# Weight block sums of two down products kept in DRAM, one pair sum moved between two taps, and the joints' order changed, in a kernel of two transformer blocks

## The reference, cut to what matters

```python
# first block (SiLU gate), then a gated per-layer embedding ("ple")
h = rms_norm(x, norm_ffn)
x = x + (silu(h @ w_ffn_gate) * (h @ w_ffn_up)) @ w_ffn_down
gate = sigmoid(rms_norm(x, norm_ple) @ w_ple_gate)
x = x + gate * (p @ w_ple_proj)
x = rms_norm(x, norm_final)
# second block (a causal depthwise convolution of 3 taps, GELU gate)
u = causal_dwconv(h2 @ w_up, conv_w, conv_b)
y = (gelu(u[..., :2816]) * u[..., 2816:]) @ w_down
```

## Time and profile before

| | us |
|---|---|
| median of 3 runs | 2708.07 (2702.29 to 2712.51) |
| the profiled execution, its own time | 2705.71 |
| its span | 2703.9 |
| PE busy | 2583.1 (96%), 11826 matmuls |
| DVE busy | 1786.3 (66%) |
| ACT busy | 1189.3 (44%) |
| POOL busy | 1199.0 (44%) |
| chain that ended last, by engine | PE 56%, DVE 22%, ACT 6%, POOL 6%, DMA 5%, issue 5% |

### The profile page before, as it was taken

The page is one execution under the profiler, slowest core; times in us unless marked ns, Lnnn a source line. Parts: engine busy times, 40 slices in busy tenths (PEclk is TensorE's granted clock), DMA queues, the critical chain, the costliest instruction groups (busy, mean ns, idle before and its releaser), DMA issues.

```text
span 2703.9 us, 32099 instructions
## 1 busy us (share of the span) xinstructions
PE 2583.1 (96%) x11826; PEld 2081.1 (77%) x11826; DVE 1786.3 (66%) x2176; ACT 1189.3 (44%) x2076; POOL 1199.0 (44%) x764
## 2 busy tenths in 40 slices
PE   7999999999899999999898999998999999999997
PEld 6887788888688888888676777877767777777875
DVE  6888876653855454589945556427378666666997
ACT  6777421122533333444454243355354444444444
POOL 2444522223455555556633311134433555554566
PEclk9999999999999999999999999999999999999998
DMA  3000044432122222565422112122321222226753
GB/s 123 24 24 24 19 149 155 153 113 109 47 79 85 86 78 94 170 232 176 144 78 89 48 31 46 32 76 69 132 86 63 78 86 71 86 78 221 253 177 132
DMA packets 119580, 271.59 MB, mean 100 GB/s; under 512 B 12664, under 2 KB 26232, under 8 KB 119296
## 3 DMA queue, kind: packets, MB, share of 16 engines
q1 hardware_dynamic: 119424, 269.54, 30.1%
HBM read 231.15 MB, written 38.34 MB: 100 GB/s over the span
## 4 chain that ended last, share of the span: by engine, by line
PE 56%; DVE 22%; ACT 6%; POOL 6%; DMA 5%; issue 5%; SPq 0%; DVEq 0%; ACTq 0%; POOLq 0%
PE psum_mem L750 20%; PE psum_mem L1045 15%; PE psum_mem L1075 4%; POOL w_lo L3958 3%; DVE tmp_mem L3672 3%; DMA w_raw<-in_w_up_b 2%; PE psum_mem L1244 2%; PE psum_mem L1249 2%; PE psum_mem L1246 2%; PE psum_mem L812 2%; DVE x_lo_a L3065 2%; DVE w_raw L2942 1%; PE psum_mem L796 1%; DVE w_raw L3048 1%; PE psum_mem L847 1%
## 5 line engine op out<-in xcount | busy, mean ns | idle before, releaser
L3958 POOL TENSOR_TENSOR w_lo<-w_raw,w_hi 128x512 fp32r<-128x512 f32 x320 | 495.9, 1555 | 464.2 <-ACT w_hi L1834 447.6
L3864 POOL TENSOR_TENSOR w_lo<-w_raw,w_hi 128x1024 fp32r<-128x1024 f32 (+2 forms) x105 | 237.4, 2261 | 624.5 <-ACT w_hi L1599 542.0
L1834 ACT CAST w_hi<-w_raw 128x512 fp32r<-128x512 f32 x320 | 196.4, 620 | 323.2 <-DMA w_raw<-in_w_up_b 72.1
L1045 PE MATMUL psum_mem<-h_hi,w_hi 128*128 128x512 f32 x672 | 266.4, 396 | 20.9 <-ACT norm_row L2470 18.2
L1045 PE MATMUL psum_mem<-h_lo,w_hi 128*128 128x512 f32 x672 | 264.0, 393 | 1.3 <-DVE h_lo L2951 1.3
L1045 PE MATMUL psum_mem<-h_hi,w_lo 128*128 128x512 f32 x672 | 263.2, 392 | 0.0
L750 PE MATMUL psum_mem<-h_hi,w_hi 128*128 128x512 f32 x736 | 232.1, 397 | 11.4 <-ACT h_hi L1633 8.9
L750 PE MATMUL psum_mem<-h_lo,w_hi 128*128 128x512 f32 x736 | 228.8, 392 | 5.7 <-DVE h_lo L3582 5.5
L750 PE MATMUL psum_mem<-h_hi,w_lo 128*128 128x512 f32 x736 | 228.3, 391 | 2.7 <-POOL w_lo L3864 2.7
L1599 ACT CAST w_hi<-w_raw 128x1024 fp32r<-128x1024 f32 (+2 forms) x105 | 100.3, 955 | 266.9 <-PE psum_mem L750 253.8
L750 PEld LDWEIGHTS psum_mem<-h_hi,w_hi 128*128 128x128 f32 x736 | 137.9, 189 | 43.4 <-ACT h_hi L1633 8.9
(11 more groups left out here) (466 smaller groups left out, 6434.1 us busy)
## 6 DMA issues: line engine op xcount, KB each, us to landing
hidden<-tmp_mem SPq DMA_DIRECT2D x44, 512.0 KB, 2.6
w_raw<-in_w_up_b SPq DMA_DIRECT2D x44, 512.0 KB, 3.7
w_raw<-in_w_ffn_down SPq DMA_DIRECT2D x77, 256.0 KB, 3.4
w_raw<-in_w_down_b SPq DMA_DIRECT2D x77, 256.0 KB, 3.2
x_ring_a<-hidden SPq DMA_DIRECT2D x66, 256.0 KB, 3.3
x_ring_b<-hidden SPq DMA_DIRECT2D x66, 256.0 KB, 3.2
w_raw<-in_w_in_a SPq DMA_DIRECT2D x32, 512.0 KB, 3.7
ada_raw<-in_w_ada SPq DMA_DIRECT2D x64, 256.0 KB, 3.3
```

Of the source, the lines that this page charges most:

```text
L1045: made = e.matmul(out, wt, x, start=j <= DIFF_3 and k == 0 and part == 0, stop=k == KH - 1 and part == 2, skip_group_check=True)
L1834: e.copy(w_slot(w_hi, slot, of), source).then_inc(*S.of("w_hi", key))
L3864: e.tensor_tensor(w_lo[:, i, 0:width], w_raw[:, i, 0:width], w_hi[:, i, 0:width].bitcast(F32), ALU.subtract).then_inc(*S.of("w_lo", c))
L3958: e.tensor_tensor(w_slot(w_lo, slot, of), source, w_slot(w_hi, slot, of).bitcast(F32), ALU.subtract).then_inc(*S.of("w_lo", key))
```

## The change

1. The weight sums of M_6, M_7, M_3 and M_5 of both down products are made during the first block's feed-forward pairs: 22 tile groups (11 for "a", 11 for "b"), one beside each of the pairs 1 to 19, two beside the pairs 1, 7 and 13. Each takes two loads of 512 KB, four DVE sums of 128x512 and one store of 1 MB to a new DRAM scratch array `down_sums`. Two DVE sums stand ahead of the pair sum, two behind the high weight sum. `keep_w`, its 22 loads and the weight part of `down_sums` are gone; the four products read their weight tiles from the array.
2. Both down products use the order M_1, M_2, M_5, M_6, M_7, M_4, M_3.
3. In the second block DVE's pair sum of pair i+1 moves between the two up taps of pair i, the high weight sum of pair i+1 behind the second tap, and the product of pair i behind that. Unit 3 of the second down product is prepared one step earlier.
4. In the joint, the ple rows are made in halves as soon as their blocks are final: first half of rows 0 to 3 beside M_6, the rest beside M_3, and the last four after it. ACT's split of p's weight tile moves behind all of these rows. The small gain vectors move to unit 15.
5. `hidden_out(KF - 1)` moves behind the weight load of unit 6, in both down products.

```diff
-DOWN_ORDER = {"a": (M_1, M_2, M_5, M_6, M_3, M_7, M_4), "b": (M_1, M_2, M_5, M_6, M_7, M_4, M_3)}
+DOWN_ORDER = (M_1, M_2, M_5, M_6, M_7, M_4, M_3)
+W_SUM = {M_6: 0, M_7: 1, M_3: 2, M_5: 3}
+SUM_TILES = [(of, kt) for of in "ab" for kt in range(KF // 2)]
+def sum_tiles_beside(i):
+    return [n for n in range(len(SUM_TILES)) if 1 + n * 19 // len(SUM_TILES) == i]
...
 ACT, first block, down product
             for u in range(2, DOWN_UNITS):
                 p, kt = divmod(u, KB)
...
-                if p == 6 and kt in (0, 2, 4, 6):
...
+                if p == 3 and kt in (0, 2, 4, 6):
+                    if kt == 0:
+                        for n in (KF - 2, KF - 1):
+                            w.wait_ge(f"hid_out{n % 2}", ("a", n))
+                    ple_row(kt // 2, 0)
+                elif p == 6 and kt < 4:
+                    ple_row(KH + kt, 1)
+                elif p == 6 and 6 <= kt < 10:
+                    ple_row(KH + kt - 6, 0)
+            for k in range(KH):
+                ple_row(k, 1)
             ahead(1)
-            for k in range(KH, KD):
-                w.wait_ge(*down_added("a", 6, k - KH))
...
 ACT, second block, pairs
                 tap_first(i, 1, up_banks(i))
+                if i == KF - 1:
+                    down_unit("b", 3)
                 gelu(i)
...
 DVE, down_sums
-                if m in W_KEPT + W_MADE:
...
-                        e.tensor_tensor(kept, kept, raw, ALU.add).then_inc(*S.of("dn_sum", (of, "w", u)))
...
 DVE, first block, pairs
+            def first_tile_sums(n):
+                low, high, late, high_late = (sum_part(n, j) for j in range(4))
+                w.wait_ge(f"in_ws{n % 2}", (n, 1))
+                e.tensor_tensor(high_late, high, high_late, ALU.add).then_inc(*S.of("ws_sum", (n, M_5)))
+                w.own("ws_sum")
+                e.tensor_tensor(high, low, high, ALU.subtract).then_inc(*S.of("ws_sum", (n, M_7)))
+
+            def last_tile_sums(n):
+                low, high, late, high_late = (sum_part(n, j) for j in range(4))
+                w.own("ws_sum")
+                e.tensor_tensor(low, high_late, low, ALU.subtract).then_inc(*S.of("ws_sum", (n, M_6)))
+                w.own("ws_sum")
+                e.tensor_tensor(late, late, low, ALU.subtract).then_inc(*S.of("ws_sum", (n, M_3)))
             for _, i in FFN_PAIRS:
+                for n in sum_tiles_beside(i):
+                    first_tile_sums(n)
...
                 b_sum(i)
...
                 weight_high_sum(i)
+                for n in sum_tiles_beside(i):
+                    last_tile_sums(n)
...
 DVE, second block, pairs
+            back_sum(PLAIN)
+            weight_high_sum(PLAIN, "b")
             for _, i in FFN_PAIRS[PLAIN:]:
-                back_sum(i)
-                weight_high_sum(i, "b")
...
-                whole_rest(i, 1, up_banks(i))
+                late_taps = tap_rest(i, 1, up_banks(i))
+                next(late_taps)
+                if i < KF - 1:
+                    back_sum(i + 1)
+                else:
+                    down_low("b", 3)
+                for _ in late_taps:
+                    pass
+                if i < KF - 1:
+                    weight_high_sum(i + 1, "b")
                 ffn_product(i)
...
 SP, w_load
+                if m in W_SUM:
+                    n = SUM_TILES.index((of, kt))
+                    w.wait_ge(f"ws_out{n % 2}", n)
+                    source = io["down_sums"][n][:, HALF * W_SUM[m]:HALF * (W_SUM[m] + 1)]
...
 SP, first block, pairs
+                for n in sum_tiles_beside(i - 1):
+                    sum_out(n)
+                for n in sum_tiles_beside(i):
+                    sum_load(n)
...
 SP, both down products
-            hidden_out("a", KF - 1)
             for u in range(4, DOWN_UNITS):
                 w_load("a", u)
+                if u == 6:
+                    hidden_out("a", KF - 1)
                 if u >= KB:
                     x_load("a", u)
-                if u < KB + 4:
-                    kept_w_load("a", u - 4)
```

More of the change, by code:

```diff
@@ L1140, in tensor @@
                 if m == 0:
-                    w.wait_ge("row_v", ("ple", 7))
-                    w.wait_ge("row_g", ("ple", (7, 1)))
+                    for half in range(NH):
+                        w.wait_ge(*ple_added(half, KD - 1))
                     sum_partitions("ple", norm_row, (("inv_m", ("ple", 1)),))
@@ L3136, in vector @@
-            e.scalar_tensor_tensor(out=gain[:, 2 * KD:3 * KD], in0=mod[:, 4 * KD:5 * KD], scalar=1.0,
-                                   in1=vec("pre_ffn_g", 0, KD), op0=ALU.add, op1=ALU.mult).then_inc(*S.of("gain", 3))
-            e.tensor_tensor(gain[:, 3 * KD:4 * KD], mod[:, 5 * KD:6 * KD], vec("post_ffn_g", 0, KD),
-                            ALU.mult).then_inc(*S.of("gain", "all"))
-            square_c, root_c, half_c, gain_c = (final_gain[:, i, :] for i in range(4))
-            e.tensor_tensor(square_c, vec("norm_final", 0, KD), vec("norm_final", 0, KD),
-                            ALU.mult).then_inc(*S.of("final_gain", "square"))
@@ L3153, in vector, with last_row_add @@
-            for k in range(KH):
-                ple_low(k)
-            for k in range(KH, KD):
-                ple_low(k, 1)
+                elif p == 3 and kt in (1, 3, 5, 7):
+                    ple_low(kt // 2, 0)
+                elif p == 6 and 1 <= kt < 5:
+                    ple_low(KH + kt - 1, 1)
+                elif p == 6 and 7 <= kt:
+                    ple_low(KH + kt - 7, 0)
+            def last_row_add(at):
+                w.wait_ge("square", ("ple", (1, PLE_ROWS[1][at])))
+                w.wait_ge(*ple_added(1, at - 1))
+                ple_row_add(e, "row_v", 1, at)
@@ L3991, in gpsimd, with ple_added_row @@
                         fill_pair(i + 1, j)
+            def ple_added_row(half, at):
+                w.wait_ge("square", ("ple", (half, PLE_ROWS[half][at])))
+                if at == 1:
+                    w.wait_ge("square", ("ple", (half, PLE_ROWS[half][0])))
+                else:
+                    w.wait_ge(*ple_added(half, at - 1))
+                ple_row_add(e, "row_g", half, at)
             for u in range(DOWN_UNITS):
@@ L3994, in gpsimd @@
                 p, kt = divmod(u, KB)
-                if p == 6 and kt in (3, 5, 7):
-                    add_square("ple", kt // 2, norm_row[:, :], tmp[:, (kt // 2 - 1) % 2, :])
-            taken[0], done[0] = ff_end, ff_end
-            for k in range(KH, KD):
-                w.wait_ge("square", ("ple", (k, 1)))
-                w.own("row_g")
-                e.tensor_tensor(norm_row[:, half_of(1)], norm_row[:, half_of(1)], tmp[:, (k - 1) % 2, half_of(1)],
-                                ALU.add).then_inc(*S.of("row_g", ("ple", (k, 1))))
+                if p == 3 and kt in (4, 6, 8):
+                    ple_added_row(0, kt // 2 - 1)
+                elif p == 6 and 3 <= kt < 6:
+                    ple_added_row(1, kt - 2)
+                elif p == 6 and 8 <= kt:
+                    ple_added_row(0, kt - 4)
+            taken[0], done[0] = ff_end, ff_end
+            ple_added_row(0, KD - 1)
             ahead(1)
```

206 lines of the change are left out of this document (101 added, 105 removed), and 3 rows, old and new, of the table SHARED.

## The result

The change makes the kernel **slower**: 2730.47 us median (2730.18 to 2732.72, 4 runs) against 2708.47 (2702.29 to 2712.51, 4 runs), ratio 1.0085 with a 95% interval of 1.0065 to 1.0105. The forecast was 2697, and its range ended at 2716.

A forecast was written before the change was run, and what follows sets the result against it. Bounds taken: TensorE's pace in the first pairs, a closed round without TensorE in the second. Terms +8 +5 -8 -9 -7 +0 = -11 against 2705.7 give 2694.7; the median lies 2.4 above, so 2697, range 2674 to 2716.

The forecast's parts named there:

- First pairs, +5 forecast: First block's pairs: added sums overrun the room by 1.6 us at pairs 1, 7 and 13; +5 (0 to +10).
- Room: 3.9 us: First pairs, before the pair sum: DVE idles 2.65 us and the pair sum may be late by another 1.3.
- They now have about 2 us to spare: First pairs: POOL's splits come up to 1.4 us later, row 0 with them, within about 2 us of slack.
- Rival 4: First pairs: tile sums stall every pair because tiles land late, 32 us instead of 5, whole 2724; chance 0.12.
- Second pairs, +8 forecast: Second block's pairs: row 0 queues behind store and row 1; +0.45 us a round, 18 pairs, +8 (-11 to +22).
- Rivals 1 and 2: Second pairs: 1, pair sum was the limit, 18.5 us less, chance 0.10; 2, row 0 not held up, -11, chance 0.12.
- the 0.96 us of UP_HIGH's low part: Second pairs: with the product moved away, POOL's low part of UP_HIGH takes 1.30 us instead of 2.26, -0.96.
- Down "a", -8 forecast: First down product: weight sums leave DVE and keep_w loads leave SP; 1.5 us loss remains, -8 (-6 to -9.5).
- First joint, 0 forecast: First joint: DVE's block goes, but ACT's split of p's weights makes a like wait; 0 (-9 to +2).
- Second joint and down "b", -16 forecast: Second joint's -7 and down "b"'s -9 taken together.
- -7: Second joint: last tile's store moved behind unit 6's load frees unit 4's load, removing TensorE's hole; -7 (-5 to -7.5).
- -9: Second down product: weight sums leave DVE and keep_w loads leave SP; 2 us loss remains, -9 (-5 to -11).

The follow-up runs named there:

- the store after the landing: Changed kernel, but the second pairs' hidden store goes behind both weight loads and waits until row 0 has landed: 2707.21 us, ratio 1.0002.
- the two edits that undo this: Changed kernel with block 20's store behind the second joint's first loads (2731.89 us), or with the second pairs' pair and high weight sums back at the head (2720.45 us).

## Why the prediction was wrong

- **First pairs, +5 forecast, +28.7 measured: the step that failed.** The prediction spends the same room twice. It says "Room: 3.9 us ... two need 1.4 to 3.6 and fit", and then, of POOL's splits and of row 0's load behind them, "They now have about 2 us to spare". But pair sum, high weight sum, DIFF_4's split, row 0's load and the next low weight sums are one circle, with one room of 3.5 to 4.0 us in all. The 3.9, worked out against TensorE's wait for the copy "two", is by luck about that size, and the two sums with 3.3 us do fit: without the transfers single intervals are back near 19.04. What the prediction put at nothing is what the sums and transfers make longer on the circle. In the interval shown row 0's load took 0.75 us more (at the median of the stage 4.6 in place of 4.3), the high weight sum 0.48 and DIFF_4's low part 0.51. That is 0.6 + 0.75 + 0.48 + 0.51 past the 2.65, against 1.34 that were left: 1.0 over, 0.92 measured. "Row 0 is issued before the new transfers, so these queue behind it" was wrong as a protection: row 0's load fell to 3.6 us without them. And the 2.65 of the earlier trace rows is the largest idle time of the stage; its median is 2.3. By intervals, the three double pairs cost about 18 us where 5 were forecast, the others about 11 where 0 was.
- **Rival 4** had the direction and a price (32 us) near the truth, and its sign came: TensorE waits for `parts` 17 times, and not at three pairs. Its mechanism was half right. The tile sums do stall every pair, at 1.66 each, and the port is part of it. But the tile does not land late: of the 22 first sums one waited for its tile (1.85 us, the second tile of pair 7), and in the interval shown the loads were issued from 1049.81 and the first sum began at 1061.23 straight behind DVE's own work.
- **Second pairs, +8 forecast, +9.3 measured: right**, by its own steps: row 1 at 4.8 (4.89), row 0 at 6.1 (6.11), from the weight sum's end to row 0 7.3 (2183.90 to 2191.17, 7.27), a round of 20.5 (20.43). Rivals 1 and 2 both fall for the kernel as changed. With the store after the landing the stage gains 16 us, near rival 1's 18.5, but by the 0.96 us of UP_HIGH's low part, which the prediction had as a term, and, as far as the traces tell, not by the pair sum.
- **Down "a", -8 forecast, -8.5 measured: right.** TensorE waits 0.8 us in all there.
- **First joint, 0 forecast: right.** The wait of 4.70 for DVE's add became one of 4.43 for ACT's split, and the steps came as worked out: TensorE resumes 4.6 us after the down product's end (forecast 4.7), makes 4 matmuls, waits for POOL until 7.2 (7.4), and p ends at 18.8 (19.3, as before). The stage between the down product and the second pairs, in which it lies, is 2.5 us shorter, within the scatter that stages without an edit show. Whether an earlier split by ACT would close the hole was not tried.
- **Second joint and down "b", -16 forecast, -2.7 measured.** Two terms failed. The joint's "-7" freed the load of unit 4, but the order of part three makes the product of pair 20 late, and SP waits for it with the store of block 20 while units 0 to 3 and the kept loads stand behind; with either of the two edits that undo this the gap is 0.2 us. I had followed the store of the last block past its queue, and not the one before it. And the "-9" did not ask how far SP runs ahead. The burst of `x_last`, which the old kernel passed without loss (43 to 45 products in each window of 10 us behind it), costs 6.4 us. When the burst went out, the trace before shows 307 products of down "b" made, the trace after 326 (a few may be missing in both), so SP's lead was 19 products, 4.3 us, shorter. The code has a reason: in M_5 and M_6 a weight slot was free as soon as DVE had made the sum, and now only when POOL has made the low part. No run changes that alone, so it stays argued; that the burst makes the hole is shown. Run by run: 8 us lost at the joint, of which the loads ahead of the store recover 4.7 once the burst is gone, and 6.4 at the burst. With both repaired the stretch takes 215.5 us, 13.9 less than before, so the "-16" was nearly there to be had.

By stages the sum misses by 23.7 us in the first pairs, 13.3 at the second joint and in down "b", 1.3 in the second pairs, less 2.8 elsewhere: 35.5 in the span, 33.5 between the medians (2730.5 less 2697). The prediction gives its own spread as -28 to +4 "by its bounds taken together"; the bounds of its terms add up to -47.5 and +18, and how they were taken together it does not say. The measured +24.5 of the span lies beyond either, because no bound of the first pairs went past +10.

## What to carry to other kernels

A gap in an engine's row is room only along every way that leads on from it. Before work is put into it, follow what stands behind it, close the circle with the next load, and add up the gaps of the whole circle once. Then set against them not only the new work but everything that the work and its transfers make longer on the circle: here 3.3 us of sums brought 1.7 us of that with them. The place that looked worse, behind the weight sum, was the free one, since there the engine waited for a transfer and its neighbour on the port was idle. And a transfer is not safe because it was issued first: what is on the circle should be landed before bulk transfers go out, which was one wait on SyncE and worth 25 us here.

## What was not expected of the hardware

- A 512 KB load took 4.76 us with a 512 KB store issued 0.37 us behind it on the same queue, where the loads took 3.6 to 3.7 at the median once the store or the tile transfers were kept away from them. I had read queue order as protection. The Trainium skill (DMA: Bandwidth & Descriptors, Queues, rings and completion order) has descriptors consumed in ring order on each DMA engine, and says in the same place that a later one may finish its write before an earlier one; the measurement is not at odds with that. Which part of the way load and store share, no run here shows.
- DVE's sum of two SBUF operands took 0.69 us with POOL idle and 1.66 beside POOL's split of 128x512, so where a sum stands changed its price by a factor of 2.4.
- Two delays that cost 0 and 11.6 us alone cost 28.7 together.
